# RWKV scan of a hybrid trunk: the triangular inversion kept in 64x64 diagonal blocks and multiplied in quarters of the array, one product fewer, the next pair's operands made ahead, the two heads' row halves alternating

## The reference

```python
def rwkv7_scan(seq, S0):
    def step(S, inp):
        r_t, w_t, k_t, v_t, a_t, b_t = inp
        sa = jnp.einsum('bhvk,bhk->bhv', S, a_t)
        S = S * w_t[:, :, None, :] + sa[..., None] * b_t[:, :, None, :] + v_t[..., None] * k_t[:, :, None, :]
        return S, jnp.einsum('bhvk,bhk->bhv', S, r_t)
```

## Time and profile before

| | |
|---|---|
| median of three runs | 4027.08 us (4021.76 to 4029.38) |
| the profiled execution's own time | 4025.17 us |
| its span | 4023.4 us |
| TensorE busy | 3296.2 us, 82% of the span |
| VectorE, ScalarE, GpSimd busy | 1837.6, 816.9, 899.4 us |
| granted TensorE clock, mean | 0.891 of full speed |

### The profile page before, as it was taken

How to read it: one execution, slowest core, us unless ns; L and a number is a source line. 1 busy time by engine, 2 the same in 40 slices (tenths; PEclk the granted TensorE clock), 3 DMA queues, 4 the chain that set the end, 5 groups by cost and what they waited for, 6 DMA issues and landing times. The chain is left out here.

```text
span 4023.4 us, 36240 instructions
## 1 busy us (share of the span) xinstructions
PE 3296.2 (82%) x12424; PEld 1966.4 (49%) x12424; DVE 1837.6 (46%) x3814; ACT 816.9 (20%) x1554; POOL 899.4 (22%) x820
## 2 busy tenths in 40 slices
PE   8798885887999999998898777677777777777776
PEld 2466773355777777776654323223232333323232
DVE  0005765434333333333313567666656656674443
ACT  0202323102222211222202111211121121112212
POOL 0000000000111111110000344344444444353442
PEclk9899997898988888989999888888888888888888
DMA  6211001021000000000513999899999999999996
GB/s 254 99 32 47 19 13 61 0 89 47 20 24 18 26 26 27 27 26 36 177 58 147 356 384 361 344 386 375 383 367 387 378 369 373 384 386 370 389 375 255
DMA packets 123496, 794.47 MB, mean 197 GB/s; under 512 B 14983, under 2 KB 16647, under 8 KB 38888
## 3 DMA queue, kind: packets, MB, share of 16 engines
q0 software_dynamic: 92160, 671.13, 42.2%
q1 hardware_dynamic: 31208, 121.62, 8.6%
HBM read 776.18 MB, written 16.52 MB: 197 GB/s over the span
## 5 line engine op out<-in xcount | busy, mean ns | idle before, releaser
L1910 PE MATMUL pr_psy<-pr_rows,pr_diag 128*128 128x512 f32 x2560 | 1312.2, 673 | 449.4 <-ACT pr_diag L1965 448.5
L1910 PEld LDWEIGHTS pr_psy<-pr_rows,pr_diag 128*128 128x128 f32 x2560 | 540.2, 217 | 1218.2 <-issue 666.8
L2092 DVE CUSTOM_DVE_ANT_0 pr_rows<-pr_rows,pr_h_tok 128x1024 f32<-128x1024 f32 x640 | 779.3, 1225 | 649.9 <-DMA pr_rows<-in_p_uv,pr_now 647.9
L1848 POOL DMA_INDIRECT pr_rows<-in_p_uv,pr_now x640 | 728.0, 1137 | 1032.1 <-PE pr_psy L1910 903.9
L1485 POOL TENSOR_TENSOR yT<-rw_sys,rw_bmask 128x640 f32<-128x640 f32 x32 | 48.6, 1542 | 1621.3 <-DVE rw_sys L1548 1621.3
L1960 ACT ACTIVATE pr_act<-pr_dot 128x4 f32<-128x4 f32 x160 | 32.8, 205 | 1328.7 <-DVEq L2096 1328.6
L1277 PE MATMUL rw_gate_ps<-hT,rw_gate_w 128*128 128x320 f32 x768 | 246.4, 458 | 0.0
L1965 ACT ACTIVATE pr_diag<-con,pr_weight 128x128 f32<-128x128 f32 x640 | 204.4, 390 | 58.2 <-DVE pr_weight L2102 55.8
L1277 PEld LDWEIGHTS rw_gate_ps<-hT,rw_gate_w 128*128 128x128 f32 x768 | 140.0, 196 | 51.7 <-issue 10.4
L1561 DVE TENSOR_TENSOR rw_X<-rw_X,rw_ring 128x640 f32<-128x640 f32 x96 | 78.8, 821 | 176.5 <-PE rw_ring L1324 176.2
L287 PE MATMUL hg_ps<-hT,hg_w 128*128 128x320 f32 x512 | 139.7, 436 | 16.8 <-DMA hg_w<-in_w_in 16.8
(11 more groups left out here) (369 smaller groups left out, 3878.3 us busy)
## 6 DMA issues: line engine op xcount, KB each, us to landing
ada_w<-in_w_ada SPq DMA_DIRECT2D x8, 3072.0 KB, 10.5
rw_gate_w<-in_w_in SPq DMA_DIRECT2D x24, 512.0 KB, 4.0
pr_rows<-in_p_uv,pr_now POOLq DMA_INDIRECT x640, 9.3
hg_w<-in_w_in SPq DMA_DIRECT2D x16, 512.0 KB, 3.5
rw_w<-in_w_in SPq DMA_DIRECT2D x15, 512.0 KB, 3.5
gate_scratch<-rw_gate SPq DMA_DIRECT2D x24, 320.0 KB, 4.0
mg_gate<-gate_scratch SPq DMA_DIRECT2D x24, 320.0 KB, 3.5
mg_wb<-in_w_branch SPq DMA_DIRECT2D x24, 256.0 KB, 2.7
```

The costliest lines, as they stand in the source:

```text
L1848: nc.gpsimd.indirect_dma_start(out=rows[:, r].rearrange("p u d -> p (u d)"), out_offset=None, in_=A["p_uv"], in_offset=bass.IndirectOffset ...
L1910: last = nc.tensor.matmul(ps_y[:, c % 2, a], diag[:, r], rows[:, r, 1, a * 512:(a + 1) * 512], start=(first and r == 0), stop=False, skip_ ...
L2092: nc.vector.tensor_tensor_reduce(out=rows[:, r, 0], in0=rows[:, r, 0], in1=h_tok[:, c], scale=1.0, scalar=0.0, op0=ALU.mult, op1=ALU.add, ...
```

## The change

- The full 128x128 inverse is no longer kept from the start. `sys_` holds `LB` and `LBT` only as the two 64x64 diagonal blocks of each matrix (one over the other in the partitions), and `OFF`, the 64 columns that hold the block off the diagonal: 576 columns instead of 640. `LBT` comes masked to 16x16 blocks, so that GpSimd makes D alone, chunk by chunk.
- All inversion steps up to J1 work on 64x64 blocks: for each chunk two matmuls, one in the quarter of the array with rows and columns 0 to 63, one in that with rows and columns 64 to 127 (`quarters`), where one 128x128 matmul stood. The last level makes one block off the diagonal (Y2, W2, J2: one quarter for each head and chunk) and writes the full inverse to `XF`. The transposes Y become float32 matmuls with the identity.
- U4 and D8 are gone; T = D4 X takes their place, and X3 adds D4 T.
- In the systems the two heads alternate matmul by matmul, chunk by chunk, in two slots of the ring. One gate matmul follows each chunk and four the last.
- `sums`, the arguments, the exponentials and the operands of pair w+1 are made during the inversion of pair w (`AHEAD`), with `AR` and `ends` doubled; the decays come after D4.
- The block of 16 gate matmuls is gone. Of the 48 of a pair, 9 follow the systems, 13 stand between inversion steps (`IN_STEPS`), 26 in the scan (`scan_share`).
- In the scan the state's product comes before Y, the heads alternate within each group, and the parts of Y and S that do not need SA are issued ahead of it. The ring's order in the scan is R1, SA, S, Y instead of R1, SA, Y, S.

The core of the diff:

```diff
-KINDS = 5
-LBT, MBR, LKT, MKR, LB = range(KINDS)
+H64 = [slice(0, HD), slice(HD, P)]
+LKT, MKR, MBR = (slice(P * n, P * n + P) for n in range(3))
+OFF, LB, LBT = (slice(3 * P + HD * n, 3 * P + HD * n + HD) for n in range(3))
+SYS_W = 3 * P + 3 * HD
...
+            own = [K.yT[b][:].rearrange("p k t -> p (k t)").rearrange("p (n h c t) -> p n h c t", n=4, h=2, c=NCH)
                    for b in range(2)]
-            D_, U_, D2, U2 = (own[n // 2][:, n % 2] for n in range(4))
+            D_, D2, U2, D4 = (own[0][:, n] for n in range(4))
+            C_, X_ = [own[1][:, n] for n in range(2)], own[1][:, 2]
+            XF = wb("XF", [P, 2, NCH, P])
...
-            STEPS = [("U2", "s"), ("D2", "v"), ("X1", "v"), ("U4", "s"), ("D4", "s"), ("X2", "v"), ("D8", "s"),
-                     ("X3", "v")]
+            FIRST = [(H64[0], H64[1]), (H64[1], H64[0])]
+            STEPS = [("U2", "s"), ("D2", "v"), ("X1", "v"), ("D4", "s"), ("X2", "v"), ("T", "s"), ("X3", "v")]
...
+                for c in range(NCH):
+                    for hh in range(2):
                         use.add((w, "sys", hh, c), "v")
...
-                if w < 7:
-                    for x in ("w", "a"):
-                        use.add((w + 1, x), "s")
+                    if (x, hh) == ("D4", 1) and w < 7:
+                        for y in ("w", "a"):
+                            use.add((w + 1, y), "s")
                 for k in range(NCH):
-                    for x in ("R1", "SA", "Y", "S"):
+                    for x in ("R1", "SA", "S", "Y"):
...
+            POOL = [("D", c) for c in range(NCH)] + [(x, hh) for x in ("X0", "C0", "C1") for hh in range(2)]
...
+            AFTER_SYS = 4
+            IN_STEPS = {"D2": 2, "D4": 2, "T": 3, "W0": 2, "W1": 2, "W2": 2}
+            PER_PAIR = 3 * 2 * KD
+            IN_SCAN = PER_PAIR - NCH - AFTER_SYS - sum(IN_STEPS.values())
+
+            def scan_share(point):
+                return IN_SCAN * (point + 1) // (3 * NCH) - IN_SCAN * point // (3 * NCH)
...
-                        gates(3 * w, 0, 2 * KD)
...
+                        first, second = FIRST[d]
+                        for c in range(NCH):
+                            outs = []
+                            for hh in range(2):
+                                use.wait_free(pe, (w, "sys", hh, c))
+                                outs.append(flat((w, "sys", hh, c)))
+                            for hh, hp in enumerate(rows_of):
+                                nc.tensor.matmul(outs[hh][:, MBR], bT[hp, c], AR[hp, c, 1], start=True, stop=True)
+                            for hh, hp in enumerate(rows_of):
+                                nc.tensor.matmul(outs[hh][:, 0:2 * P], kd[hp, c],
+                                                 AR[hp, c].rearrange("p a t -> p (a t)"), start=True, stop=True)
+                            for hh, hp in enumerate(rows_of):
+                                nc.tensor.matmul(outs[hh][:, OFF], AR[hp, c, 0], bT[hp, c, first], start=True, stop=True)
+                            for half in H64:
+                                for hh, hp in enumerate(rows_of):
+                                    nc.tensor.matmul(outs[hh][half, LB], AR[hp, c, 0, half], bT[hp, c, half],
+                                                     start=True, stop=True)
+                            for half in H64:
+                                for hh, hp in enumerate(rows_of):
+                                    last = nc.tensor.matmul(outs[hh][half, LBT], bT[hp, c, half], AR[hp, c, 0, half],
+                                                            start=True, stop=True)
+                                    if half == H64[1]:
+                                        last.then_inc(use.mm_done, 1)
+                            gates(1)
+
+                        gates(AFTER_SYS)
+
+                        def quarters(key, l, r):
+
+                            use.wait_free(pe, key)
+                            out = chunks(key, HD)
                             for c in range(NCH):
-                                key = (w, "sys", hh, c)
-                                use.wait_free(pe, key)
-                                o = flat(key)
-                                ar = AR[hp, c].rearrange("p a t -> p (a t)")
-                                nc.tensor.matmul(o[:, 0:2 * P], bT[hp, c], ar, start=True, stop=True)
-                                nc.tensor.matmul(o[:, 2 * P:4 * P], kd[hp, c], ar, start=True, stop=True)
-                                nc.tensor.matmul(o[:, 4 * P:5 * P], AR[hp, c, 0], bT[hp, c], start=True,
-                                                 stop=True).then_inc(use.mm_done, 1)
-
-                        gates(3 * w + 1, 0, BEGUN)
-                        mm = lambda l, r: (lambda o, c: nc.tensor.matmul(o, l[:, c], r[:, c], start=True, stop=True))
+                                for hp in H64:
+                                    last = nc.tensor.matmul(out[hp, c], l[hp, c], r[hp, c], start=True, stop=True)
+                            last.then_inc(use.mm_done, 1)
...
+                                use.wait_read(pe, (w, "X2", hh))
+                                quarters(key, D4h, X)
...
                             elif name == "X3":
-                                use.wait_read(pe, (w, "D8", hh))
-                                use.wait_read(pe, (w, "X2", hh))
-                                product(key, mm(D, X))
+                                use.wait_read(pe, (w, "T", hh))
+                                quarters(key, D4h, D)
...
+                            elif name == "W2":
+                                use.wait_free(pe, key)
+                                out = chunks(key, HD)
+                                for c in range(NCH):
+                                    last = nc.tensor.matmul(out[first, c], sys_[second, hh, c, OFF],
+                                                            XF[second, hh, c, second], start=True, stop=True)
+                                last.then_inc(use.mm_done, 1)
...
+                            if hh == 1:
+                                gates(IN_STEPS.get(name, 0))
...
+                            key_y, key_s = (w, "Y", k), (w, "S", k)
+                            use.wait_free(pe, key_y)
+                            out_y = flat(key_y, P)
+                            for hh, hp in enumerate(hps):
+                                nc.tensor.matmul(out_y[hp], v_of(hh), sys_[:, hh, c, MKR], start=True, stop=False)
+                            if with_state:
+                                for hh, hp in enumerate(hps):
+                                    nc.tensor.matmul(out_y[hp], STp[hp, :], AR[hp, c, 1], start=False, stop=False)
+                            gates(scan_share(3 * k + 1))
...
+                                use.wait_free(pe, key_s)
+                                out_s = flat(key_s, HD)
+                                for hh, hp in enumerate(hps):
+                                    nc.tensor.matmul(out_s[hp], kd_tok[:, c, hp], v_of(hh), start=True, stop=False)
+                            gates(scan_share(3 * k + 2))
...
+                            if k < NCH - 1:
+                                for hh, hp in enumerate(hps):
+                                    last = nc.tensor.matmul(out_s[hp], b_tok[:, c, hp], sa[hh], start=False, stop=True)
...
+                            rows = FIRST[w // 4][0] if name in ("Y2", "W2") else slice(0, P)
+                            take((w, name, hh), dst[:, hh], HD, rows)
+                            if w < 7 and (name, hh) == ("D4", 1):
+                                take_decays(w + 1)
+                            if (name, hh) == ("T", 1):
+                                take_gate(3 * w)
+                            if w < 7 and (name, hh) == ("W0", 1):
+                                exponentials(w + 1)
...
+                    AHEAD = {"X2": [sums], "X3": [arguments], "J0": [keys_of], "J1": [queries, operands]}
+                    for part in (sums, arguments, keys_of, queries, operands):
+                        part(0)```

TensorE at the start of a pair, before: what stands from the block of gate matmuls to the first chunk of the systems (`rw_ring<-A,B` has the moving operand before the weights; the shape is that of the result).

```order
L1277 MATMUL rw_gate_ps<-hT,rw_gate_w 128x320 x16
L1310 MATMUL rw_ring<-con,rw_bT 128x128 x5
L1310 MATMUL rw_ring<-con,rw_kd 128x128 x5
L1318 MATMUL rw_ring<-rw_AR,rw_bT 128x256
L1319 MATMUL rw_ring<-rw_AR,rw_kd 128x256
L1320 MATMUL rw_ring<-rw_bT,rw_AR 128x128
```

More of the change, by code:

```diff
@@ L1266, in product, with gates @@
                         last.then_inc(use.mm_done, 1)
-                    def gates(i, first, end):
-                        for n in range(first, end):
+                    emitted = [0]
+                    def gates(count):
+                        for _ in range(count):
+                            i, n = divmod(emitted[0], 2 * KD)
```

(11 more changed lines are left out.)

321 lines of the change are left out of this document (163 added, 158 removed).

## The result

The changed kernel takes 3815.2 us (median of 4, 3803.5 to 3831.4) where the kernel before takes 4024.4: a ratio of 0.948, 95% interval 0.945 to 0.952. 3796 was forecast, with 3765 to 3915 as range. The profiled execution is the one of 3803.5 us; the sum had given 3794 for it. The fastest of the four has the highest mean clock and the slowest the lowest: 0.904, 0.900, 0.900 and 0.895 for 3803.5, 3814.4, 3816.1 and 3831.4 us.

The account below looks back on a forecast made before the run. TensorE's work and waits were taken to bound the pair loop. Systems 15.1, inversion 31.7 and scan 31.7 gave 78.5 us a pair; with first and last pair, 641 against 872, so 3796 us, range 3765 to 3915.

Parts of the forecast that it names:

- the likeliest case: Whole kernel: 3796 us, with 3770 to 3825 given chance 0.60.
- product of one head, two quarters: Inversion: 5 chunks, 2 quarters, 2 passes take 0.58 us if both quarters overlap fully, 1.16 if one follows the other.
- chunk of systems: Systems of a pair: one chunk for both heads, with slot wait and gate matmul, takes 2.3 us.
- stand ahead of the first pair: Before the first pair: nothing hides its operands, 12.0 us less 1.4, so 10.6 us.
- first pair at 1.2 GHz: First pair: TensorE starts at 1.2 GHz for transposes and some three chunks, 5 us.
- slot wait behind R1: Scan: Y's slot is R1's, so TensorE waits for VectorE's copy, about 0.55 us a chunk.
- third gate tile: Scan: the third gate tile waits until ScalarE has taken the second, 0.6 us.
- rivals 1: Inversion: the two quarters take turns, 13.4 us more a pair, 107 us in all, 3903 us; chance 0.16.
- 2 (1.24): Inversion: TensorE can't be fed, 0.062 us a pass, 38.1 instead of 31.7 us a pair, 3847 us; chance 0.06.
- Rival 3: Inversion: new waits, VectorE late by 0.3 us at each of 16 steps, 38 us, 3834 us; chance 0.12.
- the idle time after which the clock fell is gone: Systems: the 3.2 us wait for bT, after which the clock fell to 1.2 GHz, goes with early operands.
- rival 4: Loop: runs at 1.2 GHz throughout with 64-row matmuls, 56 us more a pair, 4237 us, slower; chance 0.05.

Follow-up runs that it names:

- late: The changed kernel, but VectorE and ScalarE make the next pair's operands after the scan's last Y; 3886.4 us, 0.966 of the kernel before.
- in_turn: The changed kernel, but head 0's matmuls all issued ahead of head 1's in each chunk's systems, R1 and Y; 4006.6 us, 0.995 of the kernel before.
- gates_behind: The changed kernel, but the one gate matmul behind each chunk's systems goes behind the fifth chunk; 3847.7 us, 0.956 of the kernel before.
- late_in_turn: The changed kernel with operands made after the scan, gates behind the fifth chunk's systems, one head's systems behind the other's; 4030.2 us, 1.001 of the kernel before.

## Why the prediction was right, and what in it was not

The range held and the likeliest case came. By its steps, for the profiled execution:

| term | forecast | measured |
|---|---|---|
| product of one head, two quarters | 0.58 | 0.58 |
| chunk of systems | 2.3 | 2.44 |
| transposes and systems | 15.1 | 15.70 |
| inversion with 13 gates and decays | 31.7 | 31.98 |
| scan | 31.7 | 32.16 |
| pair | 78.5 | 79.84 |
| stand ahead of the first pair | 10.6 | 9.59 |
| first pair at 1.2 GHz | 5 | 1.9 (81.71 less 79.84) |
| last pair | 76.0 | 77.3 |
| slot wait behind R1 | 0.55 | 0.38 |
| third gate tile | 0.6 | 0.4 |
| loop | 641 | 649.3 |

**Prices.** The one unknown price, two quarters at once, was taken at the lower of its two bounds, and that was right to the last digit: rivals 1 (1.16 a product) and 2 (1.24) are out. It took both kinds of half from rows of before. One part no row covered, two row halves in one bank; there the lower bound was a judgement, with 0.16 against it, that came out.

**The sum** was 8 us short in the loop. Seven pairs of 1.35 more are 9.4, the clock's one fall 1.5; the first pair gave 2.8 back (1.0 of the stand, and 81.71 where 83.5 was due). Of a pair's 1.35, 0.6 is in the systems, 0.3 in the inversion and 0.45 in the scan; the first is 0.14 for each of four chunks. The trace has its source:

```profile
1104.25 1.42 DVE L1646 TENSOR_TENSOR rw_sys<-rw_ring,rw_mask 128x576 f32<-128x576 f32 x2 [2.78 <-PE rw_ring L1337]
```

The row holds both heads' reads; the first takes 0.75 us and ends at 1105.00, and the next chunk starts at 1105.15. The sum had a term for the semaphore from TensorE to VectorE, and none for the way back. Rival 3 did not come: TensorE waits for a VectorE read in the inversion only ahead of Y2, 0.8 us a pair, less than the 1.7 that the sum had for its chains. Outside the loop the time grew by 1.2 us.

**The step that failed** is not one of the sum but one under it: "the idle time after which the clock fell is gone", given as the reason against rival 4. The runs show that in the changed kernel idle time is not what keeps the clock down, and that a fall does not need it. With it back (late) the clock returned in 4 to 9 us; with it gone and heads in turn (in_turn) it fell all the same, and with the gates behind (gates_behind) too. What holds 2.4 GHz through the systems are the two other things that I had named beside it, both row halves at work and gates between; without either it fell in some or all pairs. The first pair's 5 us were too many for the same reason: with heads alternating and gates between, the clock was back after 4.7 us, a loss of 1.9. The reading of the rows had a gap as well: it took the second pair for all, and the seventh pair of before shows that the clock could come back in such systems. Rival 4 as priced, the whole loop at 1.2 GHz, came in no run. Its mechanism is nearer than 0.05 suggests: of in_turn's 191 us, 84 are lost overlap (8 times 10.5), so the clock took some 107, a quarter of the 441 of rival 4, for one loop turned round.

**What the change's parts are worth** has no single answer. From the bottom up, in medians: 4030 (late_in_turn: quarters, gates moved and the scan as changed), 3950 with heads alternating in the systems, 3886 with a gate in each chunk, 3815 with early operands: 80, 64, 71. Taken away singly from the top, alternating in the systems is worth 77 and in the scan 58 (both 191), the gates' place 32, early operands 71, issuing quarters alternately 64. What the quarters alone are worth in a kernel that holds its clock was not run.

**The median** lies 12 us above the profiled execution, where 1.9 had been assumed. The others have a lower mean clock. That they had more falls like that of the fifth pair is likely; they have no trace, so it is not shown.

## What to carry to other kernels

Before ordering small matmuls, read the granted clock over each stretch beside the waits, and in every repetition of the stretch, not in one: a stretch of half-array or quarter-array work with no idle time can run at 1.2 GHz, and two neighbouring halves with a full-array matmul between them held 2.4 here. Issue matmuls of different quarters alternately, not in runs. Matmuls with no deadline (here the gates) go where an in-order engine would otherwise wait, directly behind what it waits for; count in which group a tile of theirs gets full, since its next one waits for the copy.

## What the hardware did that I had not expected

- The array overlaps passes of different halves that are not issued alternately, but only some three passes deep: a group of 80 passes took 3.55 us up to the next gate, 2.48 when issued alternately, and about 4.8 would be no overlap.
- The clock falls without idle time, and not every time. Of in_turn's pairs two and three, with the same records, one held 2.4 GHz and the other lost 18.7 of its 109.1 us; in the kernel before, the seventh pair was 10 to 11 us shorter than the five ahead of it.
- Costs of the clock don't add: two edits of 77 and 58 us cost 191 together, though the overlaps that they lose do add (5.7 and 4.9 a pair against 10.5).
